# NSA value sums in a hybrid decoder layer: values as the stationary operand, two heads on the column halves, and probability rows scaled before their transposes

## What is computed

```python
s = where(ok, q @ k_cmp.T * scale - slope * dist, NEG_INF)      # 63 compressed keys
p_cmp = softmax(s) * ok
o_cmp = p_cmp @ v_cmp
imp = einsum('bhgqn,ns->bhqs', p_cmp, overlap)                  # picks 4 of 32 blocks
p = softmax(where(ok, q @ k_sel.T * scale - slope * dist, NEG_INF)); o_sel = p @ v_sel
p = softmax(where(ok, q @ k_win.T * scale - slope * dist, NEG_INF)); o_win = p @ v_win
o = g[..., 0:1] * o_cmp + g[..., 1:2] * o_sel + g[..., 2:3] * o_win   # sigmoid gates
```

## Time and profile before

| | us |
|---|---|
| median of 3 runs (1495.3 to 1495.51) | 1495.47 |
| the profiled execution's own time | 1493.83 |
| its span in the trace | 1492.1 |
| PE busy | 1416.8 (95%) |
| DVE busy | 673.0 (45%) |
| ACT busy | 355.2 (24%) |
| POOL busy | 471.1 (32%) |
| NSA's 96 pieces, within the span | 525 to 749 |

### The profile page before, as it was taken

How to read it: one execution, slowest core, us unless ns; L and a number is a source line. 1 busy time by engine, 2 the same in 40 slices (tenths; PEclk the granted TensorE clock), 3 DMA queues, 4 the chain that set the end, 5 groups by cost and what they waited for, 6 DMA issues and landing times.

```text
span 1492.1 us, 18380 instructions
## 1 busy us (share of the span) xinstructions
PE 1416.8 (95%) x7437; PEld 1159.1 (78%) x7437; DVE 673.0 (45%) x1053; ACT 355.2 (24%) x621; POOL 471.1 (32%) x240
## 2 busy tenths in 40 slices
PE   5799799999999899999999979999999999999998
PEld 4688467799887667777778868788888888888887
DVE  5896665525453553444445231532323232364641
ACT  5311544400101134344401010421111111231110
POOL 4324002234622110111133333334434343444542
PEclk9999999999989899999999999999999999999999
DMA  7411101031101000000012041321111111141122
GB/s 181 45 29 42 43 1 29 15 76 54 36 19 52 15 22 1 19 18 18 1 36 53 29 159 53 127 72 43 49 49 42 56 42 56 42 156 56 43 72 98
DMA packets 126821, 76.44 MB, mean 51 GB/s; under 512 B 39312, under 2 KB 113424, under 8 KB 126736
## 3 DMA queue, kind: packets, MB, share of 16 engines
q1 hardware_dynamic: 126752, 75.46, 18.0%
HBM read 66.93 MB, written 8.52 MB: 51 GB/s over the span
## 4 chain that ended last, share of the span: by engine, by line
PE 88%; DVE 5%; ACT 3%; issue 1%; DMA 1%; POOL 0%; SPq 0%; ACTq 0%; DVEq 0%; POOLq 0%
PE ps L642 23%; PE ps L643 23%; PE ps L644 23%; PE ps L1123 4%; PE ps L1153 3%; PE ps L1137 2%; PE ps L875 1%; PE ps L892 1%; PE ps L905 1%; DMA raw<-in_w_out 1%; PE ps L657 1%; PE ps L1081 1%; ACT arena L1269 1%; PE ps L1100 1%; DVE hTl L2009 1%
## 5 line engine op out<-in xcount | busy, mean ns | idle before, releaser
L554 POOL TENSOR_TENSOR wh<-raw,zero 128x1024 fp32r<-128x1024 f32 (+2 forms) x93 | 188.1, 2022 | 988.3 <-PE ps L644 950.4
L642 PE MATMUL ps<-hTh,wh 128*128 128x512 f32 x1008 | 402.8, 400 | 3.9 <-ACT arena L1344 3.1
L643 PE MATMUL ps<-hTl,wh 128*128 128x512 f32 x1008 | 395.8, 393 | 0.0
L644 PE MATMUL ps<-hTh,wl 128*128 128x512 f32 x1008 | 395.6, 392 | 0.0
L557 POOL TENSOR_TENSOR wl<-raw,wh 128x1024 fp32r<-128x1024 f32 (+2 forms) x93 | 257.0, 2763 | 7.3
L642 PEld LDWEIGHTS ps<-hTh,wh 128*128 128x128 f32 x1008 | 191.7, 190 | 43.4 <-ACT arena L1344 3.5
L644 PEld LDWEIGHTS ps<-hTh,wl 128*128 128x128 f32 x1008 | 191.1, 190 | 41.1
L643 PEld LDWEIGHTS ps<-hTl,wh 128*128 128x128 f32 x1008 | 191.7, 190 | 37.8
L642 PE MATMUL ps<-wh,hTh 128*128 128x512 f32 (+2 forms) x512 | 179.9, 351 | 7.5 <-POOL wl L557 7.5
L643 PE MATMUL ps<-wl,hTh 128*128 128x512 f32 (+2 forms) x512 | 179.6, 351 | 0.0
L644 PE MATMUL ps<-wh,hTl 128*128 128x512 f32 (+2 forms) x512 | 179.5, 351 | 0.0
(11 more groups left out here) (331 smaller groups left out, 1596.7 us busy)
## 6 DMA issues: line engine op xcount, KB each, us to landing
raw<-in_w_in SPq DMA_DIRECT2D x35, 512.0 KB, 3.9
raw<-in_w_up SPq DMA_DIRECT2D x32, 512.0 KB, 4.0
raw<-in_w_down SPq DMA_DIRECT2D x16, 512.0 KB, 3.7
merged<-in_x SPq DMA_DIRECT2D x8, 512.0 KB, 7.2
raw<-in_w_out SPq DMA_DIRECT2D x8, 512.0 KB, 3.7
merged<-in_x SPq DMA_DIRECT2D x2, 2048.0 KB, 10.3
x_keep<-merged SPq DMA_DIRECT2D x2, 2048.0 KB, 10.1
conv<-x_keep SPq DMA_DIRECT2D x1, 2048.0 KB, 8.1
```

Source lines behind the costliest of these rows:

```text
L554: eng.tensor_tensor(wh[:, p, 0:n], raw[:, p, 0:n], zero1[:, 0:1].broadcast_to((P, n)), ALU.add).then_inc(s_hi[0], 1)
L642: mm(out_, ah, bh, start=first, stop=False, skip_group_check=True)
L643: mm(out_, ah, bl, start=False, stop=False, skip_group_check=True)
L644: return mm(out_, al, bh, start=False, stop=last, skip_group_check=True)
```

## The change

1. `pv` runs only on pieces of odd heads, for both heads of the pair at once: 64 value columns are stationary, `pT` of head e streams 128 columns, and head e goes to PSUM partitions 64e to 64e+63. There is no column of ones. The two branches add into the same bank (3 or 7 by query block), so the result is already channels by queries.
2. The row sum comes from the `accum_out` of ACT's exponential. A new DVE step `scale_row` (at lag 2) adds the two partial sums, inverts, multiplies by the gate and scales the whole probability row in `prow`; `tp` now waits for `p_scaled` of the row instead of `p_exp` of the piece.
3. `branch_out`, the transposes of `o` and their copies go; one DVE addition for each query block takes their place. `pT` gets four slots instead of two.
4. In the compressed branch the gates are multiplied into `p_cmp` after the sum over heads that the choice needs, and `pc_ready` is signalled behind both; `pvc` runs on column halves, and a plain copy takes the place of the gate product.

```diff
-        LAG_EXP, LAG_T, LAG_PV, LAG_OUT = 1, 3, 4, 5
+        LAG_EXP, LAG_SCALE, LAG_T, LAG_PV, LAG_OUT = 1, 2, 3, 4, 5
             if i - LAG_EXP in ROW_END:
                 PLAN.append(("exp", ROW_END[i - LAG_EXP]))
+            if i - LAG_SCALE in ROW_END:
+                PLAN.append(("scale", ROW_END[i - LAG_SCALE]))
             if 0 <= i - LAG_T < NPC:
                 PLAN.append(("tp", i - LAG_T))
-            if 0 <= i - LAG_PV < NPC:
+            if i - LAG_PV in PV_EVEN:
                 PLAN.append(("pv", i - LAG_PV))
...
-                        ins = mm(ps[:, 3, c0:c0 + HD], pcT[n % 2][0:N_CMP, h * P:(h + 1) * P],
-                                 vcmp[0:N_CMP, 0:HD], start=True, stop=True, skip_group_check=True)
+                        ins = mm(ps[r, 3, h // 2 * P:(h // 2 + 1) * P], vcmp[0:N_CMP, 0:HD],
+                                 pcT[n % 2][0:N_CMP, h * P:(h + 1) * P], start=True, stop=True, skip_group_check=True)
...
                 elif kind == "tp":
-                    eng.wait_ge(S("p_exp"), n + 1)
+                    eng.wait_ge(S("p_scaled"), row + 1)
...
-                        ins = mm(ps[:, 7 if v % 2 else 3, h * 65:(h + 1) * 65], pT[n % 2][:, i * P:(i + 1) * P],
-                                 kv_tok[:, kb + i, vc:vc + 65], start=h == 0 and off == 0 and i == 0,
+                        for e, piece in enumerate((PV_EVEN[n], n)):
+                            ins = mm(ps[HD * e:HD * e + HD, out_bank[m % 2], h // 2 * P:(h // 2 + 1) * P],
+                                     kv_tok[:, kb + i, vc:vc + HD], pT_block(piece % 4, i),
...
-                elif kind == "o":
-                    eng.wait_ge(S("on_read"), 2 * n + 2)
-                    for c in range(2):
-                        ins = eng.transpose(ps[:, 1, c * P:(c + 1) * P], oacc[:, n, c * P:(c + 1) * P], ident[:, :])
...
                             eng.activation(prow[n % 2][:, off * P:(off + nb) * P], ps[:, 4 + i % 3, 0:nb * P], ACT.Exp,
-                                           bias=neg_max[:, n % 8:n % 8 + 1]).then_inc(S("p_exp"), 1)
+                                           bias=neg_max[:, n % 8:n % 8 + 1], accum_out=den[:, d:d + 1]
+                                           ).then_inc(S("p_exp"), 1)
...
-                ins.then_inc(S("pc_ready"), 1)
-                eng.wait_ge(S("pc_ready"), hb + 1)
+                then(ins)
...
                 then(eng.tensor_reduce(php[:, :, 1:1 + N_CMP], pcmp.rearrange("p n h c -> p n c h"), AX.X, ALU.add))
+                for i in range(4):
+                    ins = tt(pcmp[:, i], pcmp[:, i], over(gates[:, 4 * hb + i, 0:12:3].unsqueeze(2), (P, NH, N_CMP)), ALU.mult)
+                ins.then_inc(S("pc_ready"), 1)
...
-            def branch_out(n, br):
...
-                then(eng.reciprocal(rden, src[:, :, one:one + 1].rearrange("p h o -> p (h o)")))
-                then(tt(coef, rden, gates[:, n, (1 if br == "sel" else 2):12:3], ALU.mult))
-                for h in range(NH):
-                    o = oacc[:, n, h * HD:(h + 1) * HD]
-                    ins = stt(o, src[:, h, d0:d0 + HD], coef[:, h:h + 1], o, ALU.mult, ALU.add)
...
+            def scale_row(row):
+
+                m, br, h, end = ROWS[row]
+                d, k = den[:, 2 * (row % 4):2 * (row % 4) + 2], row % 4
+                one, r, c = d[:, 0:1], rden[:, k:k + 1], coef[:, k:k + 1]
+                eng.wait_ge(S("p_exp"), end + 1)
+                if PIECES[end][3]:
+                    then(tt(one, d[:, 0:1], d[:, 1:2], ALU.add))
+                then(eng.reciprocal(r, one))
+                g = 3 * h + (1 if br == "sel" else 2)
+                then(tt(c, r, gates[:, m, g:g + 1], ALU.mult))
+                w = (PIECES[end][3] + PIECES[end][2]) * P
+                ts(prow[row % 2][:, 0:w], prow[row % 2][:, 0:w], c, None, ALU.mult).then_inc(S("p_scaled"), 1)
...
+                elif kind == "scale":
+                    scale_row(n)
                 elif kind == "o":
...
+                    tt(mixT[:, :, t], mixT[:, :, t], ps[:, out_bank[n % 2], 0:2 * P].rearrange("p (c q) -> p c q", c=2),
+                       ALU.add).then_inc(S("on_read"), 1)
```

More of the change, by code:

```diff
@@ L325, in program @@
         ROW_END = {end: row for row, (n, br, h, end) in enumerate(ROWS)}
-        V_END = {end: (n, br) for n, br, h, end in ROWS if h == NH - 1}
+        PARTNER = {(ROWS[row][:3], kb): i for i, (row, kb, nb, off) in enumerate(PIECES)}
+        PV_OPS = [i for i, (row, *rest) in enumerate(PIECES) if ROWS[row][2] % 2]
+        PV_EVEN = {i: PARTNER[ROWS[PIECES[i][0]][:2] + (ROWS[PIECES[i][0]][2] - 1,), PIECES[i][1]] for i in PV_OPS}
+        PV_COUNT = {}
+        for count, i in enumerate(PV_OPS):
+            PV_COUNT[i] = PV_COUNT[PV_EVEN[i]] = count + 1
+        N_END = {end: n for n, br, h, end in ROWS if h == NH - 1 and br == "sel"}
         FILLS = 100
@@ L367, in program @@
             rest = rest[take:]
-        T_ITEMS = [op for op in PLAN if op[0] in ("tp", "o")]
         def n_bank(g):
@@ L1142, in _ @@
                     m, br, h = ROWS[row][:3]
-                    v = 2 * m + (br == "sel")
                     eng.wait_ge(S("pT_read"), n + 1)
-                    if h == 0 and off == 0:
-                        if v >= 2:
-                            eng.wait_ge(S("on_read"), v - 1)
+                    if br == "win" and h == 1 and off == 0:
+                        if m >= 2:
+                            eng.wait_ge(S("on_read"), m - 1)
                         else:
@@ L1990, in _ @@
                     row_max(n)
[L1991 to L1999 removed]
+                elif kind == "scale":
+                    scale_row(n)
+                elif kind == "o":
+                    end = {m: i for i, m in N_END.items()}[n]
+                    eng.wait_ge(S("pv_nsa"), PV_COUNT[end])
+                    eng.wait_ge(S("cmp_out"), TB)
+                    t = slice(n * P, (n + 1) * P)
+                    tt(mixT[:, :, t], mixT[:, :, t], ps[:, out_bank[n % 2], 0:2 * P].rearrange("p (c q) -> p c q", c=2),
+                       ALU.add).then_inc(S("on_read"), 1)
+            eng.wait_ge(S("on_read"), TB)
             eng.wait_ge(S("prod"), prod_after[P_SBMERGE + 7])
             for k in range(2):
[L2002 to L2005 removed]
+                then(eng.tensor_copy(br_h[:, k, :], mixT[:, k, :]))
+                tt(br_l[:, k, :], mixT[:, k, :], br_h[:, k, :].bitcast(F32), ALU.subtract).then_inc(S("br_ready"), 1)
             def mixed_low(j):
```

81 lines of the change are left out of this document (33 added, 48 removed).

## The result

| | before | after |
|---|---|---|
| median of 4 runs each, us | 1495.49 (1495.3 to 1499.2) | 1598.77 (1594.46 to 1600.71) |
| the profiled execution's own time, us | 1493.83 | 1598.26 |
| its span, us | 1492.1 | 1596.5 |
| PE busy | 1416.8 (95%) | 1441.7 (90%) |
| granted clock, mean of 2.4 GHz | 0.978 | 0.950 |

The ratio is 1.068 (95% interval 1.0653 to 1.0708): 6.8% slower, 103 us. I had predicted 1558 us with a range of 1520 to 1590; the measurement lies 9 us above the range. The direction and the new wait were right, the size was 41 us short, most of it because the sum put the fall of PE's clock at nothing.

What follows compares the result with a forecast made beforehand. PE's order and pace were taken to bound the stage, DVE having slack on average. -15 - 5.9 + 66.6 - 1.9 + 12 + 4.5 - 2 + 4 = +62.3 on 1493.8, plus 1.6, gave 1558 us, range 1520 to 1590.

Steps and rivals of the forecast that it cites:

- What bounds the kernel: In the two-piece stage PE's order and pace set the time; DVE's average slack doesn't decide: PE busy 156.2 of 161.0 us.
- Value sums, -15: Value sums on column halves: record spacing 0.055 instead of 0.105 us, plus 0.24 a group; 55.4 us become 40.5.
- rival (a): Scaling is early enough, PE hardly waits and the gains stand alone: 1471 us, down to 1460; chance 0.08.
- The new wait, +66.6 for 31 rows: Two-piece rows: PE's transposes wait for DVE's scaling behind the reduce, 1.93 us a window row; +66.6 us, bounds 50 and 80.
- POOL, +12 for four splits: POOL's splits hold up DVE's chain ahead of PE four times before the stage's end, 3 us each: +12.
- One-piece rows, +4.5: 32 pieces, 525 to 588 us: PE has one step of work to cover the scaling chain; +4.5 us, bounds -5 and +10.
- Compressed branch, -2: Later `pc_ready` stalls PE 1.4 us, eight `pvc` groups lose about 0.45 each; net -2 us, bounds -6 and +4.
- The end, +4: After the last fill, the next work starts about 10.8 us later instead of 6.8: +4, bounds -3 and +6.
- The clock, at nothing in the sum: Late stage: the sum had no term for a lower PE clock, which was at the upper level throughout from 588 to 749 us.
- rival (c): New waits also lower PE's clock, two of three costing up to 1.7 us each: 34 us, 1592 in all; chance 0.15.
- Rival (b), half the waits: The new waits cost about half, or one-piece rows and POOL cost nothing: 1525 us; chance 0.15.
- Rival (d), column halves that don't overlap: Value sums: a strided `pT` slot prevents overlap, 528 records of 0.105 us again: 1575 us; chance 0.03.

Runs made afterwards that it cites:

- no_scale: The changed kernel without DVE's scaling of the rows, PE's transposes waiting for the exponential as before: 1490.41 us, ratio 0.9971.
- before_wait: The kernel before with only the new chain on DVE and the wait of PE's transposes for it added: 1615.04 us, ratio 1.0804.
- fill_lag1_fused: The changed kernel with fills ahead of the transposes, scaling one step earlier and the gate product taken into the scaling: 1499.34 us, ratio 1.0033.
- no_scale_fill: no_scale with each step's fill moved ahead of its transposes: 1480.41 us, ratio 0.991.

## Why the prediction was right and where it failed

**What bounds the kernel: right.** PE's order sets the stage, and average slack on DVE decided nothing: DVE is busy 135.6 of 329.5 us in after, 41%, while PE waits for it.

**Value sums, -15: about right as work, wrong as time.** The spacing is as forecast: 32 records in 1.97 us in no_scale are (1.97 - 0.27) / 31 = 0.055. With the transposes of o, PE's busy time fell by 12.0 us where I had 15 + 1.8. But alone this work moved the time by only 5 us, against the 25 that rival (a) put on all gains (1471 forecast, 1490 in no_scale). I counted a shorter PE stream as shorter time without asking what the removed work had covered, namely ACT's round trip over the one transpose bank. Under the new wait, where before_wait and after can be compared, all gains together gave 16 us.

**The new wait, +66.6 for 31 rows: right.** In the late stage PE waited 73.6 us for the scaling in 32 waits. Less the four at splits (5.50, 5.35, 5.05, 6.50) that is 51.2 in 28, 1.83 each. The recorded wait leaves out the mask's end (1.84 - 0.06 = 1.78 of path where 1.63 is recorded), so it is about 1.98 each, 61 us for 31 rows. before_wait shows that this wait is the cause.

**POOL, +12 for four splits: right.** At the four ahead of the end PE waited 4.51, 5.50, 5.35 and 5.05 us, 20.4 in all. In the three late rows the usual recorded 1.83 comes off, in the one-piece row nearly nothing: about +14. This is read from the trace only; no run took the splits away.

**One-piece rows, +4.5: right in kind.** Their idle time grew by 7.2 us (11.2 against 62.8 - 58.8 = 4.0), of which one split is 4.5. The stretch as a whole grew by 12.0, the rest being clock.

**Compressed branch, -2: right in the sum.** The stage starts at 523.2 instead of 525.4. At the upper clock a group of `pvc` took 0.65 us, and 1.10 before (at 496.66): the 0.45 that I had put. The 1.94 of the earlier trace rows are at the lower clock, where it is 1.12 now. The stall of 1.4 us didn't show, because PE came late itself: the fills ahead of this branch ran at the lower clock until 497.5, so that the net of -2 is in part luck.

```profile
499.75 0.65 PE L1108 MATMUL ps<-arena 63*64 63x128 f32 x8 [0.24 <-ACT arena L1422]
```

**The end, +4: short by 2.5.** From the start of POOL's split to the next work it takes 852.73 - 839.48 = 13.25 us instead of 6.78, +6.5. The 2.5 are the clock again: two rounds of transposes took 1.11 and 1.09 us instead of 0.66, the last value sums 3.55, and 1.97 in no_scale.

**The clock, at nothing in the sum: the step that failed.** The busy time is 39.2 us longer (241.8 against 202.6, same stream), some 34 without the masks' ends, which the sum has in its 1.93 a row. Adding 34 to 1558 gives 1592, and 1598.8 was measured; which terms make up the last 7 isn't settled. I had the mechanism as rival (c), from one row of before in which a wait of 1.63 us was followed by 0.52 of the clock, with 34 us as its price and 0.15 as its chance. The price was good (1592 against 1599). The chance and the place in the sum were not. Against the fall I held only that the clock was at its upper level in a stage that had next to no such waits, which is no evidence on what waits do. The trace of before has rows on both sides: a wait of 2.16 us also had a group at the lower clock behind it, and a wait of 3.08 us had not, as the fill behind it starts at full pace (0.50 us for its first matmul, where after has 0.79 at the lower clock, at 491.38):

```profile
491.12 0.50 PE L642 MATMUL ps<-hTh,wh 128*128 128x512 f32 x1 [3.08 <-ACT arena L1344]
```

That called for a term between nothing and 34 us. The rival's picture was also off: it isn't two waits of three that cost 1.7 us each. Behind every wait at a split the clock was down, behind the one that ended at 617.87 for at least 15 us. Behind the single waits it fell in some rows and not in others, and the length of the wait didn't decide: it fell behind one of 1.63 us at 798.30 and not behind one of 2.23 at 819.82.

**Rival (b), half the waits: fell.** The waits were all there. **Rival (d), column halves that don't overlap: fell,** by the spacing. The announced signs all came: waits over 65 us, 32 of about 2 us, reduces right behind the masks, no PE work for over 4 us at splits, PEclk under 1.00.

**What stays open.** Why the clock is low from 526 to 541 us in some kernels (0.58 in after, 0.54 in fill_lag1_fused and in no_scale_fill) and not in no_scale, whose work there is alike, wasn't settled, nor what decides behind which of the short waits it falls. Two transpose banks, which would attack the waits for ACT, and a form in which POOL's splits avoid the rows' ends, weren't tried; nor does any run give the splits' price apart.

## What to carry to other kernels

Before moving a small step of one engine onto the path of another, count from the last thing it needs of the waiting engine: the chain behind that must be shorter than the work that the waiting engine has in between, whatever the average load says. If it isn't, each recurrence costs what is left of the chain and, in this kernel, some 0.4 to 0.6 of that again in PE's clock. Put independent work (here the fills) right ahead of such a wait, not behind it; in the kernel before, which has next to no such waits, the same move cost 13 us. And a shorter stream on the bounding engine counts only after asking which round trips the removed work had hidden.
